# The last gate's rows made during the linear attention, with the later modulation weights loaded into nine places

## The reference, cut to what matters

```python
mod = silu(cond) @ w_ada + b_ada           # w_ada is 1024 x 6144
shift_a, scale_a, gate_a, shift_f, scale_f, gate_f = split(mod, 6)
h = rmsnorm(x, norm_mix_g) * (1 + scale_a) + shift_a
proj = h @ w_in                            # q, k, v, g, decays, u
o = gated linear attention(q, k, v, decays), both directions, times silu(g)
p = multi-scale pooling(u) @ w_pool
x = x + gate_a * (concat[o, p] @ w_out)
h = rmsnorm(x, norm_ffn_g) * (1 + scale_f) + shift_f
probs = softmax(h @ w_router); gate_vals, tok_idx = top_k(probs.T, cap)
for 16 experts: ye = (silu(xe @ w_gate) * (xe @ w_up)) @ w_down * gate_vals
x = x + gate_f * scatter_add(ye);  y = rmsnorm(x, final_norm_g)
```

## Time and profile before

| what | before |
|---|---|
| median of 3 runs | 1740.54 us |
| lowest and highest run | 1737.47 and 1741.93 us |
| profiled execution, its own time | 1739.62 us |
| its span from first to last instruction | 1737.5 us |
| PE busy | 1672.4 us (96%) |
| VectorE busy | 375.6 us (22%) |
| ScalarE busy | 185.3 us (11%) |
| mean rate of the DMA engines over the span | 362 GB/s |

### The profile page before, as it was taken

One profiled execution on the slowest core, in us unless ns is written; L12 is line 12 of the kernel. 1 busy time (PEld: TensorE's weight loads), 2 busy tenths in 40 slices (PEclk: granted clock), 3 DMA queues, 4 the chain that ended last, 5 costly groups with the idle time before them and its releaser, 6 DMA issues.

```text
span 1737.5 us, 43008 instructions
## 1 busy us (share of the span) xinstructions
PE 1672.4 (96%) x19754; PEld 1036.3 (60%) x19754; DVE 375.6 (22%) x695; ACT 185.3 (11%) x295; POOL 135.3 (8%) x204
## 2 busy tenths in 40 slices
PE   6998879799999999999999999999999999999997
PEld 3787558433434356666666666666668787444443
DVE  5431573611111102020202020202020111111113
ACT  4331451200000000000000000000000000000001
POOL 1000020120101010101000000000000001010000
PEclk9999989799999999999999999999999999999999
DMA  8620842999999999999999999999999999999995
GB/s 314 218 79 1 301 150 108 366 389 416 407 417 408 416 408 417 408 416 408 416 408 415 410 410 414 400 416 399 412 403 412 396 416 398 419 399 418 395 418 243
DMA packets 123341, 628.22 MB, mean 362 GB/s; under 512 B 11197, under 2 KB 14098, under 8 KB 106794
## 3 DMA queue, kind: packets, MB, share of 16 engines
q1 hardware_dynamic: 111872, 598.74, 85.3%
q0 software_dynamic: 10256, 23.91, 4.7%
q10 hardware_dynamic: 1050, 2.97, 0.4%
HBM read 609.37 MB, written 16.21 MB: 360 GB/s over the span
## 4 chain that ended last, share of the span: by engine, by line
PE 87%; DMA 6%; DVE 3%; ACT 1%; issue 1%; SPq 1%; ACTq 0%; DVEq 0%; POOLq 0%
PE bank L1782 48%; PE bank L1794 17%; PE bank L1796 8%; DMA ring<-in_w_e_up 3%; PE bank L1369 3%; PE bank L1370 3%; PE bank L1371 3%; DMA ring<-in_w_e_gate 1%; PE bank L1396 1%; SPq L444 1%; PE bank L1681 1%; DMA raw<-in_w_out 0%; PE bank L1391 0%; DMA pos_col<-in_pos 0%; DVE S L1093 0%
## 5 line engine op out<-in xcount | busy, mean ns | idle before, releaser
L1782 PE MATMUL bank<-ring,xe 128*32 128x352 f32 x12288 | 917.6, 460 | 5.2 <-DVE xe L1293 3.1
L1782 PEld LDWEIGHTS bank<-ring,xe 128*32 128x32 f32 x12288 | 557.7, 110 | 359.4 <-issue 160.9
L1794 PE MATMUL bank<-ring,hidT 128*32 128x512 f32 x2816 | 385.5, 592 | 0.0
L1796 PE MATMUL bank<-ring,hidT 128*32 128x256 f32 x2816 | 235.4, 379 | 0.0
L1796 PEld LDWEIGHTS bank<-ring,hidT 128*32 128x32 f32 x2816 | 129.5, 110 | 172.6 <-issue 172.6
L1300 DVE TENSOR_TENSOR hid<-sg,bank 128x1056 f32<-128x1056 f32 x32 | 40.1, 1255 | 829.9 <-PE bank L1782 829.9
L1794 PEld LDWEIGHTS bank<-ring,hidT 128*32 128x32 f32 x2816 | 127.4, 110 | 29.3 <-issue 2.5
L881 ACT ACT_TABLE_LOAD x16 | 20.5, 1283 | 867.4 <-PE bank L1782 867.4
L643 POOL DMA_INDIRECT acc_dram<-yab,idx_s x15 | 24.3, 1622 | 1028.9 <-DVE yc L1311 1028.9
L1309 DVE SCALAR_TENSOR_TENSOR yab<-bank,gate_cur,gfab 128x512 f32<-128x512 f32 x16 | 12.0, 751 | 330.4 <-PE bank L1796 330.4
L881 ACT ACTIVATE sg<-bank 128x1056 f32<-128x1056 f32 x32 | 33.6, 1051 | 420.6 <-PE bank L1782 420.5
(11 more groups left out here) (262 smaller groups left out, 772.3 us busy)
## 6 DMA issues: line engine op xcount, KB each, us to landing
ring<-in_w_e_gate SPq DMA_DIRECT2D x128, 1408.0 KB, 25.2
ring<-in_w_e_up SPq DMA_DIRECT2D x128, 1408.0 KB, 25.0
ring<-in_w_e_down SPq DMA_DIRECT2D x96, 1536.0 KB
ring<-in_w_e_down SPq DMA_DIRECT2D x32, 1024.0 KB
raw<-in_w_ada SPq DMA_DIRECT2D x16, 1024.0 KB, 6.2
raw<-in_w_in SPq DMA_DIRECT2D x8, 1024.0 KB, 5.5
ada_f<-in_w_ada SPq DMA_DIRECT2D x4, 1024.0 KB, 16.5
raw<-in_w_out SPq DMA_DIRECT2D x4, 1024.0 KB, 8.4
```

What stands on the lines that cost most here:

```text
L1782: last = nc.tensor.matmul(bank[b][32 * g:32 * g + 32, 0:GCOLS], xe[:, t, c, :], w[:, n, GCOLS * g:GCOLS * g + GCOLS], start=c == 0, stop=c ...
L1794: nc.tensor.matmul(bank[6][r:r + 32, :], hidT[:, ph, t, c, :], w[:, n, 512 * h:512 * h + 512], start=first, stop=stop)
L1796: last = nc.tensor.matmul(bank[7][32 * g:32 * g + 32, 0:256], hidT[:, ph, 2, c, :], w[:, n, 256 * g:256 * g + 256], start=first, stop=stop)
```

## The change

The weights of the blocks 10 and 11 are no longer loaded by `fill(2)`. They stand in `PRE` behind block 9, so that `w_out` comes four loads later in the queue. The modulation halves from the fourth on go into six places of their own, `ada_l`, which lie over `w_hi` and `w_lo` (free between the input and the output projection); with the three slots of `raw` these are nine places. `LATE_PLACES` says which of the six each load takes. PE makes the rows of both blocks ahead of `o_rows(0)`, ScalarE copies them to `modrow`, which then stays as it is, and `o_rows(0)` waits for these copies. `gate_rows` is gone from the end of the front part, on PE and on ScalarE. In the ring's fill, slot 11 is now the sixth, and the wait for `grow_ps` is gone.

```diff
-PRE += [("ada", b, kh) for b in range(ADA_FIRST, ADA_SPLIT) for kh in range(2)]
+PRE += [("ada", b, kh) for b in range(ADA_FIRST, ADA_BLOCKS) for kh in range(2)]
...
+SPLIT_SLOTS = (3, 4, 5, 8, 9, 10)
+
+LATE_PLACES = (0, 1, 2, 3, 4, 5, 0, 1, 2, 4, 5, 1, 2)
...
 def pre_slot(n):
 
-    return FRONT_SLOTS[n] if n < FRONT else (n - FRONT) % PRE_RING
+    if n < FRONT:
+        return FRONT_SLOTS[n]
+    if ADA0 + PRE_RING <= n < WOUT0:
+        return SPLIT_SLOTS[LATE_PLACES[n - ADA0 - PRE_RING]]
+    return (n - (FRONT if n < WOUT0 else WOUT0 - (ADA0 - FRONT))) % PRE_RING
...
+def split_user(slot):
+
+    return [n for n in range(ADA0) if PRE[n][0] == "win" and pre_split(n) == SPLIT_SLOTS.index(slot) % SPLIT][-1]
...
-EXP_SLOTS = (0, 1, 8, 9, 10, 4, 7, 5, 6, 2, 3, 11)
+EXP_SLOTS = (0, 1, 8, 9, 10, 11, 4, 7, 5, 6, 2, 3)
...
             if b < ADA_FIRST:
                 return bank[5 + place_of(b) % 2]
+            if b >= ADA_SPLIT:
+                return bank[3 if b == ADA_SPLIT else 0]
             return bank[1 + 2 * (b % 2)]
...
                     elif last:
                         sp.wait_ge(lo_done, split_count(last[-1]))
+                    elif pre_slot(n) in SPLIT_SLOTS:
+                        sp.wait_ge(unit_used, split_count(split_user(pre_slot(n))))
...
                 elif n == 2:
-                    sp.wait_ge(wo_ps, 2 * T_LAT)
-                    for q in range(4):
-                        b, kh = divmod(q, 2)
-                        c0 = (ADA_SPLIT + b) * 512
-                        load(ada_raw[:, (q + 2) % 4, :].rearrange("p (k n) -> p k n", k=4), rows(w_ada[0, kh * 512:(kh + 1) * 512, c0:c0 + 512]), ada_in[q])
                     sp.wait_ge(unit_used, NSPLIT)
-                elif n == 7:
+                elif n == 8:
                     sp.wait_ge(x2_n, TILES)
                     sp.wait_ge(acc_out, 16 * (TILES + 1))
-                elif n == 9:
+                elif n == 10:
...
-                elif n == 11:
-                    sp.wait_ge(grow_ps, 2)
...
             nc.scalar.copy(mrows[:, :], bank[6][0:48, 0:P]).then_inc(mod_row, 1)
+            mod_rows(ADA_SPLIT)
+            mod_rows(ADA_SPLIT + 1)
             o_squares((0, 1))
...
-            for h in range(2):
-                gate_rows(h)
...
+            for b in range(ADA_SPLIT, ADA_BLOCKS):
+                for kh in range(2):
+                    ada(b, kh)
             pe.wait_ge(scan_done, HP)
+            pe.wait_ge(mod_row, ADA_BLOCKS + 1)
             o_rows(0)
...
-            gate_rows(0, 0)
-            gate_rows(0, 1)
             turn_row(T_LAT)
-            gate_rows(1, 0)
             logits(T_LAT)
-            gate_rows(1, 1)
             pe.wait_ge(r_pr, TILES)
```

More of the change, by code:

```diff
@@ L226, in build @@
         ada_f = [at(f"ada_f{q}", [P, UNIT], F32, SPL + (q % 2 * SPLIT + q // 2) * UNIT * 4) for q in range(4)]
+        ada_l = [at(f"ada_l{q}", [P, UNIT], F32, SPL + q * UNIT * 4) for q in range(2 * SPLIT)]
         pos_col = at("pos_col", [P, 512], F32, SPL + 40 * KB)
@@ L255, in build @@
         wrtS = at("wrtS", [P, 2, KD, EXPERTS], F32, wza_at)
-        ada_raw = at("ada_raw", [P, 4, UNIT], F32, DR)
-        gate_row = at("gate_row", [P, 2, 512], F32, modrow_at)
         xg = at("xg", [P, ROW_TILES, 256], F32, L0)
@@ L316, in ada_unit, with pre_place @@
             return b - 1 if b < ADA_FIRST else ADA0 + 2 * (b - ADA_FIRST)
+        def pre_place(n):
+            slot = pre_slot(n)
+            return ada_l[SPLIT_SLOTS.index(slot)] if slot in SPLIT_SLOTS else raw[:, slot, :]
         def ada_count(b, kh):
@@ L354, in build @@
         small_in, up_in, state_in, xs_out, x_back, fin_in = map(sem, ("small_in", "up_in", "state_in", "xs_out", "x_back", "fin_in"))
-        raw_full = {n: sem(f"raw_full{n}") for n in sorted({pre_slot(n) for n in range(NPRE)})}
-        ring_full = [sem(f"ring_full{n}") for n in range(RING)]
+        raw_full = [sem(f"raw_full{n}") for n in range(RING)]
+        ring_full = raw_full
         xg_in = [sem(f"xg_in{t}") for t in range(ROW_TILES)]
@@ L382, in build @@
         ada_in = [sem(f"ada_in{q}") for q in range(4)]
-        gate_bias, grow_ps, grow_sb, x2_rc = map(sem, ("gate_bias", "grow_ps", "grow_sb", "x2_rc"))
+        gate_bias, x2_rc = map(sem, ("gate_bias", "x2_rc"))
         primed = sem("primed")
@@ L419, in ring_need @@
         def ring_need(j, i):
-            return 16 * (j // RING + 1) + i * (16 * (EXP_UNITS // RING))
+            return 16 * (pre_loads(EXP_SLOTS[j % RING], NPRE) + j // RING + 1) + i * (16 * (EXP_UNITS // RING))
         def unit(j, i):
@@ L460, in _ @@
                         sp.wait_ge(lo_done, split_count(last[-1]))
+                    elif pre_slot(n) in SPLIT_SLOTS:
+                        sp.wait_ge(unit_used, split_count(split_user(pre_slot(n))))
                     else:
                         sp.wait_ge(w0_l, 1)
-                load(raw[:, pre_slot(n), :].rearrange("p (k n) -> p k n", k=4), pre_source(n),
+                load(pre_place(n).rearrange("p (k n) -> p k n", k=4), pre_source(n),
                      raw_full[pre_slot(n)])
@@ L603, in gather @@
                     in_offset=bass.IndirectOffsetOnAxis(ap=idx, axis=0)).then_inc(xg_in[t], 16)
-            pool.wait_ge(grow_ps, 2)
+            pool.wait_ge(unit_used, NSPLIT)
             pool.wait_ge(idx_sb, 1)
@@ L871, in _ @@
             exps(T_LAT)
-            def gate_rows(h):
-                act.wait_ge(grow_ps, h + 1)
-                nc.scalar.copy(gate_row[:, h, :], bank[2 + h][:, :]).then_inc(grow_sb, 1)
             def silu(ph, i):
@@ L1414, in ada @@
                     pe.wait_ge(raw_full[pre_slot(n)], 16 * (pre_loads(pre_slot(n), n) + 1))
-                    w = raw[:, pre_slot(n), :]
+                    w = pre_place(n)
                 spread(ada_bank(b), w.rearrange("p (k n) -> p k n", k=4), kh).then_inc(ada_used, 1)
@@ L1682, in logits @@
                 nc.tensor.matmul(out, ident[0:2, st:st + 1].broadcast_to([2, P]), brow[:, :], start=False, stop=True).then_inc(lg_ps, 1)
[L1684 to L1692, removed]
             every = range(4)
@@ L1760, in _ @@
             last.then_inc(idx_ps, 1)
-            pe.wait_ge(grow_sb, 2)
             pe.wait_ge(parts_set, 1)
             for h in range(2):
-                last = nc.tensor.matmul(bank[6][64 * h:64 * h + 64, :], parts_of[:, LAT:LAT + 1].broadcast_to([P, 64]), gate_row[:, h, :], start=True, stop=True)
+                last = nc.tensor.matmul(bank[6][64 * h:64 * h + 64, :], parts_of[:, LAT:LAT + 1].broadcast_to([P, 64]), modrow[:, h, :], start=True, stop=True)
             last.then_inc(gate_ps, 1)
@@ L1768, in _ @@
                 last = nc.tensor.matmul(bank[7][32 * q:32 * q + 32, 0:256], parts_of[:, CTX:CTX + 1].broadcast_to([P, 32]),
-                                        gate_row[:, q // 2, q % 2 * 256:q % 2 * 256 + 256], start=True, stop=True)
+                                        modrow[:, q // 2, q % 2 * 256:q % 2 * 256 + 256], start=True, stop=True)
             last.then_inc(gate_ps, 1)
```

## The result

| what | before | changed |
|---|---|---|
| median of 8 runs | 1741.24 us | 1745.77 us |
| lowest and highest run | 1737.47 and 1743.87 us | 1743.30 and 1746.78 us |
| profiled execution, its own time | 1739.62 us | 1745.43 us |
| its span | 1737.5 us | 1743.5 us |

The ratio is 1.0026, with a 95% interval of 1.0017 to 1.0036: 4.5 us slower (3.0 to 6.3).

A forecast was written before the change was run, and what follows sets the result against it. PE bounds until 1456 us, then the ring's transfers; the end follows the first expert's start one to one. Terms 4.9 + 2.3 - 1.0 - 1.1 = +5.1 us gave 1745.2 us, range 1739 to 1750.

The forecast's parts named there:

- The load, +4.9: First load of `w_out`, now behind four more loads: lands at 214.3 us instead of 209.4, +4.9 us (bounds +0.7 to +5.6).
- estimate of 212.6 us: Landing of the first `w_out` load by the skill's transfer price: +3.2 instead of +4.9, whole sum 1.7 us smaller.
- The clock, +2.3: PE's pooling and transposes behind a wait of 10 us run at half clock, +2.3 us (1.5 to 3.4).
- The gate's products, 0: Last gate's products ahead of `o_rows`: they and their copies end 1.6 us ahead of the scan, costing 0.
- `o_rows` at full clock, -1.0: PE's wait before `o_rows` closes from 4.2 to 2.3 us, so its half-clock loss goes: -1.0 us (0 to -1.9).
- The logits, -1.1: End of the front part: last logits no longer wait for the third half of `gate_rows`, -1.1 us (at most -2.54).
- The fill, 0: Ring's fill without the 4 MB of `ada_raw` and with slot 11 earlier ends at the same time: 0.
- the pause at 361 us: Transfers pause some 2 us behind the ring's fill, waiting for the first expert; forecast to shrink by 1.1 us, not vanish.
- the main case: The terms as summed, +5.1 us; with its bounds it spans 1740 to 1749 us; chance 0.76.
- A: Rival: the `w_out` load isn't late (lands at 210.1 us) or has slack; -1.4 us, 1739 us; chance 0.11.
- B: Rival: PE stays at half rate through `w_pool` products, gate's products and `o_rows`; +9.3, 1749.4 us; chance 0.09.
- C: Rival: transfers bound everything from 302 us on, so 4.2 MB less saves 10 us; about 1735 or 1730 us; chance 0.04.

## Why the prediction was right, and where its parts were not

The forecast of 1745.2 us stands 0.6 us from the median of 1745.77. The mechanism is the one forecast: the first load of `w_out` is late, PE waits long and resumes at half clock, and the end takes over the shift of the first expert. The experiment with the load first shows the cause, that with PE kept busy the clock's share. But the sum was closer than its terms, and in part that is luck: in the traces the load's term was 1.4 us too small and the shift of the first expert 2.5 us, and the time between the first expert and the 13th load, which the sum didn't have, gave half of that back.

**The load, +4.9.** *The step that failed is "it lands at 204.7 + 9.6 = 214.3 us".* The issue was forecast at 204.7 us and came at 203.80, since this execution was 1 us early throughout (`gla_3` at 200.37 instead of 201.33 us). The transfer took 11.93 us, not 9.6: +6.33 us in the traces, +7.3 counted from `gla_3`. I had priced the small loads at 0.7 us as an upper bound, and they cost 1.1 to 1.5. The rest, some 0.9 us against the third load of the earlier trace rows (10.46 us without them), doesn't come from the small loads. That row's train, issued from 45.99 us on, began with nothing in flight (the DMA share was 0.00 from 42 to 46 us), the changed one behind a modulation half that was issued at 199.64 us and landed at 204.8 us. The two loads ahead of `w_out`, issued at 202.53 and 203.39 us, took:

```profile
ada_l<-in_w_ada SPq DMA_DIRECT2D x1, 1024.0 KB, 6.6
ada_l<-in_w_ada SPq DMA_DIRECT2D x1, 1024.0 KB, 8.4
```

The first two loads of that train, issued at 45.99 and 46.85 us, took 5.4 and 7.3 us. So the loads ahead of `w_out` were already 1.1 to 1.2 us slower, which is as much as the third lacks. No run takes away the load in flight, so this share is read from the traces and not tested. The Trainium skill (DMA: Bandwidth & Descriptors, Queues, rings and completion order) says that completion isn't first in, first out within an issuing engine. The trace agrees. SP's issues, and then the times to landing:

```profile
203.80 0.80 SPq L466 DMA_DIRECT2D raw<-in_w_out  x1
204.64 0.58 SPq L492 DMA_DIRECT2D gfab<-in_b_ada  x1
```

```profile
raw<-in_w_out SPq DMA_DIRECT2D x1, 1024.0 KB, 11.9
gfab<-in_b_ada SPq DMA_DIRECT2D x1, 128.0 KB, 9.2
```

The bias load, issued 0.84 us behind `w_out`, landed at 213.8 us, 1.9 us ahead of it. The prediction's estimate of 212.6 us was 3.1 us early. It took the price of the Trainium skill (DMA: Bandwidth & Descriptors, Anatomy of one DMA) for one transfer; the skill gives that price for DMAs issued from GpSimd, and these are issued by SP.

**The clock, +2.3.** It cost 2.50 us in the trace and 2.5 us in the experiment. The wait was 12.48 us instead of 10; the half rate covered the whole of the third tile's pooling (and 0.12 us of the transposes), nearly what the bound of 3.4 us assumed. But that is one draw of several: in the run without the gate's products, the same program up to there, the tile took 4.33 us behind a wait of 12.23 us, so there the clock cost 1.3 us.

**The gate's products, 0.** *The step "Two blocks' matmuls took 1.90 us" is wrong.* The row has x16 records, but one block's two halves, 8 matmuls in the code, leave 16 records in this trace: the row is one block, and so the prediction itself read it in its paragraph on the load. The two blocks took 3.64 us (x32). With the two copies the products were then bound to end at about the scan's end and not 1.6 us ahead of it, and so they do: `o_rows` is released by ScalarE's copy 0.25 us behind the scan. The cover is gone, where I had a margin; it cost 0.2 us.

**`o_rows` at full clock, -1.0.** It gave 1.53 us in the traces. The experiment without the products shows the reason: they fill PE's wait, and without them the same span takes 2.4 us more. The Trainium skill (TensorE: Matmul & The Clock Gate, What's actually happening) has PE's clock fall when it is idle and return when it is busy; here a wait of 4.17 us was followed by 1.22 us for the first product of `o_rows`, one of 0.80 us by 0.68 us.

**The logits, -1.1.** VectorE's wait fell by 1.12 us and the way to the gather by 1.13. Whether the end moves by as much was not resolved.

**The fill, 0.** The gain is nothing, as forecast, but in *"the pause at 361 us shrinks by 1.1 us and is not used up"* the first half failed: the fill started 8.9 us later and the 13th load only 6.4, so 2.5 us went. How much is left depends on the column: by the share 3.00 x 0.08 = 0.2 us, by the rate (286 GB/s instead of the 411 of the earlier trace rows) 0.9 us. It is small, and the experiment with the late gather shows that it was not used up. Had the first expert started a microsecond earlier with the same fill, the end might not have followed it; that was not tried.

**What I didn't have.** Two things that cancel. One is +1.27 us between `o_rows` and the last product by `w_out`, most of it in the transposes at 254.83 us (3.45 us for sixteen records; with the last four 3.89 us, and 2.82 or 2.83 in the kernel before and in all the experiments). The granted clock was 0.51 from 255 to 258 us. In no other run did the clock fall on these transposes, so this belongs to the one execution. The other is -1.25 us between the first expert's start and the 13th load: 12.61 us instead of 13.86, since less of it ran at half clock (the mean granted clock there was 0.86 instead of 0.78). In the experiments that stretch took 12.4 to 13.5 us, so how much of it belongs to the change stays open.

So the "first expert 5 us later, at 353 to 354 us" came at 356.4 us (+7.6), of which 1.6 us was gone again at the end of the experts. The terms of the traces give +6.0, the medians +4.5, the forecast was +5.1.

**The rivals.** The low end of the main case was summed wrong: its terms give +0.7 + 1.5 - 1.9 - 2.5 = -2.2 us, 1738 us and not 1740. A falls: the load is late, and nothing had slack for it. B falls: the products by `w_pool` took 3.67 us, the full-clock time. C falls by the experiment that gives the 4 MB back. The direction it named, faster, was to be had at another place of the queue.

## What to carry to other kernels

Before a load is put ahead of others in a queue, ask which of those is on the chain; here one load's place was worth 0.85%, and nothing else in the change came near it. Price a load by its place in a train of loads, ask whether the train begins on an idle queue, and count what is issued behind it too. Work that fills a wait of PE of about 4 us can pay for itself by the clock: count the records of a row against the matmuls in the code before dividing its time.

## What the runs showed of the hardware

Small loads that were issued behind a 1 MB load delayed its landing: 11.59 to 11.93 us in five profiles with six of them behind it (2 of 128 KB, 4 of 32 KB), 10.46 us in one profile with two loads of 1 MB there instead.

The granted clock is not the same in two executions of the same instructions. The kernel before ran its third pooling tile in 2.99 us behind the wait at 210 us, with the clock at 1.00; with the same program up to that place another execution took 4.57 us. Behind the long wait of the changed order the tile took 5.49 us in three executions and 4.33 us in a fourth. A row from one profile doesn't say that a wait of that length is safe.
